# Token numbers summed before slot weights, and the first expert rows gathered inside the routing block

## What is computed

```python
yp = yp + mp @ w_out[l]                       # output projection, residual
...
x = h.reshape(-1, D_MODEL)                    # h = rmsnorm(yp, norm_ffn)
g_logits = (x @ w_group).astype(jnp.float32) + b_group.astype(jnp.float32)
_, g_idx = lax.top_k(g_logits, 1)             # one group of 4 experts
e_logits = ((x @ w_router).astype(jnp.float32) + b_router.astype(jnp.float32)
            ).reshape(-1, N_GROUPS, EXPERTS_PER_GROUP)
e_val, e_idx = lax.top_k(e_in, TOP_K)         # two experts of that group
e_w = jax.nn.softmax(e_val, axis=-1) * g_w
...
hid = jax.nn.silu(jnp.einsum('nd,edf->nef', x, w_gate)) * jnp.einsum('nd,edf->nef', x, w_up)
y = jnp.einsum('nef,efd->nd', hid * combine, w_down)
```

## Time and profile before

| what | us |
|---|---|
| median of 3 runs | 1143.67 (1143.56 to 1144.16) |
| the profiled execution | 1144.6 |
| its span, first to last instruction | 1142.8 |
| PE busy in the span | 1045.4 (91%) |
| DVE busy | 595.7 (52%) |
| POOL busy | 147.3 (13%) |

### The profile page before, as it was taken

The page is one execution under the profiler, slowest core; times in us unless marked ns, Lnnn a source line. Parts: engine busy times, 40 slices in busy tenths (PEclk is TensorE's granted clock), DMA queues, the critical chain, the costliest instruction groups (busy, mean ns, idle before and its releaser), DMA issues. The chain is left out here.

```text
span 1142.8 us, 16349 instructions
## 1 busy us (share of the span) xinstructions
PE 1045.4 (91%) x5907; PEld 853.6 (75%) x5908; DVE 595.7 (52%) x978; ACT 481.9 (42%) x749; POOL 147.3 (13%) x136
## 2 busy tenths in 40 slices
PE   4999999999899997988999559999999999999990
PEld 3779999999766655646888448888888778888870
DVE  4421350110266664434355655665589967458845
ACT  5431110111466663433333343455467745437534
POOL 0000000000100000001000031222224342323320
PEclk9999999999999998989999779999999999999995
DMA  6416121102530006666333566568799977869766
GB/s 214 129 48 253 56 56 56 30 28 78 137 138 1 2 1 236 227 245 205 111 113 123 198 239 207 190 229 294 234 375 380 367 253 262 292 199 367 248 197 239
DMA packets 95873, 207.31 MB, mean 181 GB/s; under 512 B 12560, under 2 KB 34873, under 8 KB 95787
## 3 DMA queue, kind: packets, MB, share of 16 engines
q1 hardware_dynamic: 88332, 179.89, 44.1%
q0 software_dynamic: 7488, 26.71, 8.8%
HBM read 175.75 MB, written 37.08 MB: 186 GB/s over the span
## 5 line engine op out<-in xcount | busy, mean ns | idle before, releaser
L605 PE MATMUL bank<-xT_hi,w_hi 128*128 128x384 f32 (+1 forms) x432 | 94.7, 327 | 0.0
L605 PE MATMUL bank<-xT_rest,w_hi 128*128 128x384 f32 (+1 forms) x432 | 93.9, 326 | 0.0
L605 PE MATMUL bank<-xT_hi,w_rest 128*128 128x384 f32 (+1 forms) x432 | 93.9, 325 | 0.0
L2238 PE MATMUL y<-down_hi,hidT_hi 128*128 128x512 f32 x192 | 77.2, 402 | 2.2 <-ACT hidT_hi L2085 2.2
L2203 PE MATMUL gate<-gate_hi,rowsT_hi 128*128 128x512 f32 x192 | 77.4, 403 | 0.7 <-ACT rowsT_hi L2060 0.7
L2204 PE MATMUL gate<-gate_rest,rowsT_hi 128*128 128x512 f32 x192 | 78.0, 406 | 0.0
L1871 DVE TENSOR_TENSOR down_rest<-w_down,down_hi 128x2048 fp32r<-128x2048 f32 x32 | 71.8, 2285 | 10.3 <-ACT down_hi L1866 9.4
L2204 PE MATMUL up<-up_rest,rowsT_hi 128*128 128x512 f32 x192 | 75.7, 394 | 0.0
L1871 DVE TENSOR_TENSOR gate_rest<-w_gate,gate_hi 128x2048 fp32r<-128x2048 f32 x32 | 73.0, 2283 | 4.7 <-ACT gate_hi L1866 4.7
L2203 PE MATMUL up<-up_hi,rowsT_hi 128*128 128x512 f32 x192 | 75.3, 392 | 0.0
L2239 PE MATMUL y<-down_rest,hidT_hi 128*128 128x512 f32 x192 | 75.1, 391 | 0.0
(11 more groups left out here) (310 smaller groups left out, 2089.4 us busy)
## 6 DMA issues: line engine op xcount, KB each, us to landing
w_gate<-in_w_gate SPq DMA_DIRECT2D x16, 2048.0 KB, 13.1
w_up<-in_w_up SPq DMA_DIRECT2D x16, 2048.0 KB, 13.7
w_down<-in_w_down SPq DMA_DIRECT2D x16, 2048.0 KB, 14.8
stage<-in_w_in SPq DMA_DIRECT2D x6, 1536.0 KB, 7.1
k_cache<-in_cache_b_k SPq DMA_DIRECT2D x8, 768.0 KB, 7.2
bias_scratch<-bias_one_row SPq DMA_DIRECT2D x1, 5800.0 KB
mixT<-in_x_prompt SPq DMA_DIRECT2D x8, 512.0 KB, 4.4
x<-in_x_prompt SPq DMA_DIRECT2D x8, 512.0 KB, 4.4
```

Of the source, the lines that this page charges most:

```text
L605: ins = nc.tensor.matmul(bank[3 * (n % 2) + i][:, 0:m], w_tiles(wt, n // CH + 1)[:, k, cols], xt[:, k, c:c + m], start=(k == 0 and x == 0) ...
L2238: nc.tensor.matmul(y[j][:, :], hidT_hi[:, k, :], moe.hi["down"][half][:, k, cols], start=(k == 0), stop=False)
```

## The change

Four things are edited. The gather of the first block's rows moves from the start of `experts` to the end of POOL's code in `mix_out`; it reads its row numbers straight from column 0 of `slot_ids` and lands in the tile of the mixed heads, which is no longer needed by then. The one-hot tables are built so that the token numbers come first: PE sums the numbers (36 matmuls of 32 columns) and then, in a second pass, the weights; the multiplication by the weights moves behind the three `row_pick` instructions, and `slot_ids` is made ahead of the small instructions for `ends`. The first half of `up_rest` moves into `mix_out`, behind these, and the second half behind the first block's low parts. And `SELECT_AFTER` moves the middle `select` from tile 5 to tile 6, with three tiles in it instead of two, so that the final one has three instead of four.

```diff
     PAIRS = NB // 2
+    gathered, first_rows = keep["gathered"], keep["first_rows"]
...
-        SPLIT_AFTER, SELECT_AFTER = (2, 4), {3: (0, 3), 5: (3, 5)}
+        SPLIT_AFTER, SELECT_AFTER = (2, 4), {3: (0, 3), 6: (3, 6)}
...
+            pool.wait_ge(mix_rest_made, TT)
+            pool.wait_ge(h_stored[0], 16 * 5)
+            pool.wait_ge(h_stored[1], 16 * 4)
+            pool.wait_ge(spare_stored, 32)
+            pool.wait_ge(slotted, TT // 3 + 2)
+            nc.gpsimd.sem_inc(consts, 1)
+            nc.gpsimd.indirect_dma_start(out=first_rows, out_offset=None, in_=io["h"],
+                                         in_offset=bass.IndirectOffsetOnAxis(ap=slot_ids[:, 0:1], axis=0)).then_inc(gathered, 16)
...
-            select(5, TT)
+            select(6, TT)
...
-            step(nc.vector.tensor_tensor(block_pick[:, :, :, 0, :], iota_p[:, 0:MAXB].unsqueeze(1).unsqueeze(1).to_broadcast(all_slots),
+
+            step(nc.vector.tensor_tensor(block_pick[:, :, :, 1, :], iota_p[:, 0:MAXB].unsqueeze(1).unsqueeze(1).to_broadcast(all_slots),
                                          block_f[:, :, :].unsqueeze(3).to_broadcast(all_slots), ALU.is_equal))
-            step(nc.vector.tensor_tensor(block_pick[:, :, :, 1, :], block_pick[:, :, :, 0, :],
-                                         weight[:, :, :].unsqueeze(3).to_broadcast(all_slots), ALU.mult))
-            step(nc.vector.tensor_tensor(block_pick[:, :, :, 0, :], block_pick[:, :, :, 0, :],
+            step(nc.vector.tensor_tensor(block_pick[:, :, :, 0, :], block_pick[:, :, :, 1, :],
                                          token_no[:, :].unsqueeze(2).unsqueeze(2).to_broadcast(all_slots), ALU.mult))
             for t in range(0, TT, 3):
                 part = [P, 3, 2, P]
...
+            nc.vector.tensor_tensor(block_pick[:, :, :, 1, :], block_pick[:, :, :, 1, :],
+                                    weight[:, :, :].unsqueeze(3).to_broadcast(all_slots), ALU.mult).then_inc(slotted, 1)
+            dve.wait_ge(slots_summed, 1)
+            numbers = y[0][0][:, 0:MAXB]
+
+            step(nc.vector.tensor_scalar(occupied[:, :], numbers, 0.0, spare_no[:, 0:1], ALU.is_equal, ALU.mult))
+            nc.vector.scalar_tensor_tensor(out=slot_ids[:, 0:MAXB], in0=occupied[:, :], scalar=-1.0, in1=numbers,
+                                           op0=ALU.add, op1=ALU.add).then_inc(slotted, 1)
+            step(nc.vector.memset(slot_ids[:, MAXB:], 0))
             step(nc.vector.memset(ends_f[:, 0:1], 0.0))
             step(nc.vector.scalar_tensor_tensor(out=ends_f[:, 1:NE + 1], in0=first_slot[:, :], scalar=1.0 / P, in1=blocks[:, :],
                                                 op0=ALU.mult, op1=ALU.add))
             step(nc.vector.tensor_scalar(ends_f[:, NE + 1:NE + 2], ends_f[:, NE:NE + 1], -1.0, None, ALU.add))
             step(nc.vector.tensor_copy(ends[:, :], ends_f[:, :]))
-            step(nc.vector.memset(slot_ids[:, MAXB:], 0))
-            dve.wait_ge(slots_summed, 1)
-            numbers = y[0][0][:, 0:MAXB]
-
-            step(nc.vector.tensor_scalar(occupied[:, :], numbers, 0.0, spare_no[:, 0:1], ALU.is_equal, ALU.mult))
-            step(nc.vector.scalar_tensor_tensor(out=slot_ids[:, 0:MAXB], in0=occupied[:, :], scalar=-1.0, in1=numbers,
-                                                op0=ALU.add, op1=ALU.add))
-            step(nc.vector.tensor_copy(slot_w[:, 1:], y[0][0][:, MAXB:2 * MAXB]))
+            moe.split_rest(dve, "up", 0, 0, 0)
+            dve.wait_ge(slots_summed, 2)
+            step(nc.vector.tensor_copy(slot_w[:, 1:], y[0][1][:, 0:MAXB]))
...
-            for t in range(TT):
-                if t % 3 == 0:
-                    pe.wait_ge(slotted, t // 3 + 1)
-                for k in range(2):
-                    for rows in (slice(0, P // 2), slice(P // 2, P)):
-                        ins = nc.tensor.matmul(y[0][0][rows, 0:2 * MAXB], row_pick[:, t, k, rows],
-                                               block_pick[:, t, k, :, :].rearrange("p v x -> p (v x)"),
-                                               start=(t == 0 and k == 0), stop=(t == TT - 1 and k == 1))
-            ins.then_inc(slots_summed, 1)
+            for v in range(2):
+                if v:
+                    pe.wait_ge(slotted, TT // 3 + 1)
+                for t in range(TT):
+                    if v == 0 and t % 3 == 0:
+                        pe.wait_ge(slotted, t // 3 + 1)
+                    for k in range(2):
+                        for rows in (slice(0, P // 2), slice(P // 2, P)):
+                            ins = nc.tensor.matmul(y[0][v][rows, 0:MAXB], row_pick[:, t, k, rows], block_pick[:, t, k, v, :],
+                                                   start=(t == 0 and k == 0), stop=(t == TT - 1 and k == 1))
+                ins.then_inc(slots_summed, 1)
...
-        gathered = p.sem("gathered")
+        gathered, first_rows = keep["gathered"], keep["first_rows"]
...
-            sp.wait_ge(gathered, 16)
+            sp.wait_ge(rows_ready, 1)
...
             def gather(b):
 
-                if b is not FIRST:
+                if not (type(b) is int and b == 1):
                     pool.wait_ge(rows_ready, b)
                 nc.gpsimd.tensor_copy(row_id[:, :], slot_ids[:, bass.ds(b, 1)]).then_inc(gather_id, 1)
-                pool.wait_ge(gather_id, b + 1)
+                pool.wait_ge(gather_id, b)
                 nc.gpsimd.sem_inc(begun, 1)
                 nc.gpsimd.indirect_dma_start(out=landing[:, :], out_offset=None, in_=io["h"],
                                              in_offset=bass.IndirectOffsetOnAxis(ap=row_id[:, :], axis=0)).then_inc(gathered, 16)
 
             nc.gpsimd.sem_inc(y_free, 1)
-            gather(FIRST)
             gather(1)
...
                     dve.wait_ge(turned, 2 * b)
                 dve.wait_ge(gathered, 16 * b + 16)
-                nc.vector.tensor_copy(rows[:, :], landing[:, :]).then_inc(rows_ready, 1)
+                nc.vector.tensor_copy(rows[:, :], first_rows if b is FIRST else landing[:, :]).then_inc(rows_ready, 1)
...
-            for c in range(2):
-                moe.split_rest(dve, "up", 0, 0, c)
             fetch(FIRST)
             rows_lo(FIRST, 0)
             rows_lo(FIRST, 1)
+            moe.split_rest(dve, "up", 0, 0, 1)
             fetch(1)
...
+        keep["gathered"] = p.sem("gathered")
+        keep["first_rows"] = keep["mixT"][:, 0, 0:D]
```

## The result

The changed kernel takes 1144.21 us (median of 20 runs), the kernel before 1141.95 beside it (20 runs): a ratio of 1.0025, with a 95% interval of 1.0016 to 1.0035, or +2.85 us (1.8 to 4.0). That is slower, as forecast (the sum had +2.4 us), and clear of noise; whether it is by more than the prediction's border of 0.2% is not, since the interval begins at 0.16% and the two medians differ by 2.26 us. The range, 1142.0 to 1148.6, holds the time. The forecast of 1146.1 lies 1.9 us above it, because its base, the kernel before, took 1143.67 us in three runs and takes 1141.95 in twenty. The profiled execution took 1143.94 us (span 1142.2), the one of before 1144.6.

The account below looks back on a forecast made before the run. One path was taken to set the time: last projection tiles, last select, slots, gather, first rows. +2.96 - 0.5 - 0.76 - 2.19 + 2.9 = +2.4 us on 1143.67 gave 1146.1 us, range 1142.0 to 1148.6.

Parts of the forecast that it names:

- The middle select: End of the projection: three tiles' select ahead of tile 7's add on DVE delays PE's turn of tile 7, +2.96 us.
- The last select and the weights: Slot chain on DVE: three tiles instead of four, -0.5 us; weights' multiplication moved behind row_pick, under PE's sum, -0.76 us.
- The first sum pass: PE's slot sum: as many instructions with half the columns take as long as the whole sum before, 0 us.
- The gather: From slot_ids to rows: 9.49 us becomes 7.3, POOL's DMA instruction still held by up_rest's half, -2.19 us.
- The clock: PE behind the stall at tile 7: granted clock falls to 0.50 for the long low stretch, +2.9 us.
- rival (a): Clock stays low through turn, router and projection: +2.3 us more, 1148.4 us; chance 0.18.
- Edits at no cost: Start of the experts: up_rest's second half, expert 1's loads, the earlier second gather and the clock at first matmuls cost 0.
- (c): At the gather, POOL comes ahead of up_rest or isn't held: -2.2 us, 1143.9 us; chance 0.13.
- (d): The clock doesn't fall behind the stall at tile 7: -2.9 us, 1143.2 us; chance 0.07.
- (e): The middle select isn't on the path, so neither stall nor clock loss comes: 1140.2 us; chance 0.06.
- (b): Behind the stall at tile 7 the clock is low only for the short stretch: -1.5 us, 1144.6 us; chance 0.10.

Follow-up runs that it names:

- sel_back: The changed kernel with the select table of before (middle select behind tile 5's copy, two tiles; four in the last): 0.9977 of the kernel before.
- sel_only: The kernel before with only the select table changed (middle select behind tile 6's copy, three tiles; three in the last): 1.0075 of the kernel before.
- pool_free: The changed kernel with both halves of up_rest behind the first rows' low parts, none ahead of the barrier: 1.0007 of the kernel before.
- no_drain: The changed kernel whose routing block ends without draining POOL's transfers, the first gather on its own semaphore: 1.0030 of the kernel before.
- filled: The changed kernel with 12 unused 512-column matmuls on PE ahead of the turn of tile 7: 0.9996 of the kernel before.
- best1: The changed kernel, middle select back behind tile 5's copy, tile 5's select in DVE's gap, no drain, up_rest's first half behind the barrier: 0.9952 of the kernel before.

## Why the prediction was right, and where its steps were off

**The middle select.** +2.96 in the sum, +2.97 in the trace (9.24 - 6.27); every wait and every instruction of that step stands in the rows of after. sel_back and sel_only show that the loss comes from it.

**The last select and the weights.** -0.5 and -0.76 in the sum. From its first instruction to the memset behind it the last select takes 3.37 us after (645.11 to 648.48), 3.86 in the earlier trace rows: -0.49. From that memset to the start of `row_pick` it is 7.88 us before and 7.10 after: -0.78.

**The first sum pass.** 0 in the sum, +0.42 in the trace. The pace was read right: at the low level 64 instructions of 64 columns take 3.44 us in sel_only (652.26 to 655.70), 144 of 32 columns 7.89 us in after, that is 0.054 and 0.055 us each. What was not reckoned with is the clock, which rises before the one sum has ended, in before for its last 0.8 us and in sel_only for its last 0.3, and stays at 0.50 through both passes in all ten traces that have two. So `row_pick` to `slot_ids` takes 5.59 to 5.60 us in these ten, 5.17 before and 5.57 in sel_only. Whether the split keeps the clock low, or whether it rises at that place by chance, isn't shown.

**The gather.** -2.19 in the sum, -1.81 in the trace. POOL was held as reckoned (its instruction ends 4.10 us after `slot_ids`; I had 4.1), which pool_free shows the other way round. The 0.38 that is missing is the end of the block: from the instruction to the copy it takes 3.58 us instead of the 3.20 of the earlier trace rows, and no_drain gets 0.39 of it back. I had written that the barrier "is through by 5 us and not late", counting POOL's instruction and not its transfer; that step failed.

**The clock.** +2.9 in the sum, +4.9 in the traced execution (turn, router and second part: 7.85 us later at their end, 2.97 of it the stall), where another 0.34 is lost up to the last select, with the clock low in tile 8's turn and router too; and 3.3 over the runs, as after minus filled (0.29%, good to some 0.2%). Four of the five traces with the stall and no filling have turn, router and projection low nearly whole, as rival (a) said, and sel_only in part. So the mechanism was right. Its size is not settled: the runs can't tell the forecast's 2.9 from rival (a)'s 5.2, and in the traced execution rival (a) is what one sees. There the terms make 2.97 - 0.49 - 0.78 + 0.42 - 1.81 + 5.2 = +5.5 us at the first gate, twice the forecast. That the total came out near +2.4 all the same is in part luck: the runs show less than that gate does.

**Edits at no cost.** Here a step was wrong. I wrote that the second gather starts earlier and that the copy waiting for it "is not late before either". It did not start earlier, because of the block's end; and the chain behind that copy was the limit before already: `hid` starts 17.98 us behind `rows` before and 17.80 after, and PE waited for it both times (0.21 and 1.50 us). That cost little in itself, since PE's wait is longer after because it came sooner through the first gate (the clock, which I left at 0 there, stays low for some 3 us from the first expert matmul on, before for some 6); but it takes away what PE gains there. The loads for expert 1, put at nothing, are the next limit behind it, as no_drain shows.

**The rivals.** (c) falls: up_rest came first by 0.26 us and held POOL. (d) and (e) fall with the rows of after. (b) was not seen in any of these traces at this place.

The terms as measured are 2.97 - 0.49 - 0.78 + 0.42 - 1.81 + 3.3 (the clock, over the runs) = +3.6 us, inside the measured 1.8 to 4.0. Since the 3.3 is itself a difference to after, what this really tests is the rest: without the 3.3 the terms give +0.3, where filled has -0.5 (-2.5 to +1.6). What stays open is how the low stretches are spread over executions: only one of each kernel is traced.

## What to carry to other kernels

Before a row of small instructions is moved out of the last place on one engine, look which wait of PE it now stands ahead of: a select that costs 3 us there and saves 0.5 at the end also costs the clock behind it. Price a stall on PE with the matmuls behind it at the low level, and look for an idle gap that takes a piece of the work (here one tile's select, 2.2 us of DVE). And a gather that is issued ahead of a barrier isn't free of it: the engine that issued it may hold the barrier until it has landed, and what comes next from the same engine then starts no sooner.

## What the runs showed of the hardware

- The end of a block waits for POOL's indirect DMA to land (the rows are copied 3.20 us after the instruction's end where nothing else holds them): 3.64 us from its instruction's end to POOL's next one in after, 0.14 us without the drain (664.59 to 664.73).
- A POOL copy of one column takes 0.18 us alone (no_drain), 0.68 beside DVE's copy of the rows (after) and 2.28 beside a half of up_rest (best1); beside DVE it ends within 0.05 us of DVE's instruction.
- Twelve unneeded matmuls (2.88 us) in a wait of PE that had been 2.81 us kept the clock at 1.00 and took 3.3 us off the kernel, good to some 2.3.
- At the low level the matmul instructions of the slot sums take as long with 32 columns as with 64: 0.055 us each (144 in 7.89 us, after) and 0.054 (64 in 3.44 us, sel_only).
